# An attention step on one core: scores of block n+2 moved ahead of the values product and the fold

## The chip, the cores and the metric

One core of one Trainium2 chip runs the whole program. The metric is the device time of one execution in microseconds; the median of three executions is 4254.33 us (4252.37 to 4255.28).

## What is computed

Two layers of a hybrid transformer block over 256 context tokens and 1024 latent tokens, width 1024: an input projection, three groups of heads (retention; latent attention, MLA, with 4 heads; grouped-query attention, GQA, with 6 query heads), an output projection, and a gated MLP. The change lies in the two kinds of attention. For each head and each block of 128 queries both compute

```python
s = jnp.einsum('bkgqd,bksd->bkgqs', qi, k).astype(F32) * scale
p = jax.nn.softmax(s, axis=-1).astype(v.dtype)
return jnp.einsum('bkgqs,bkse->bkgqe', p, v)
```

Latent queries see all 1280 keys; context queries see the 256 context keys. In the second (last) layer the context queries are left out.

## The kernel before

`attention` (L489) is called four times: MLA and GQA in each layer. It goes through heads in pairs and through the query blocks of each head, one block of 128 queries at a time, numbered n = 0 to N-1. N is 40 for MLA and 60 for GQA in the first layer (ten blocks per head, the first two of them context blocks with 256 keys), and 32 and 48 in the second (eight blocks per head, all with 1280 keys). That makes 180 blocks, 160 of them with 1280 keys. The operands are split into a high and a low part of type fp32r to keep the precision, so the scores take three matmuls per piece of keys in MLA and two in GQA.

The life of a block n, with the engine and the line:

- **scores** (PE, L554): up to three pieces of 512, 512 and 256 keys into the PSUM buffer S[n % 2]. Each piece waits on `lo_done` of block n-2, whose last reader of the same buffer is `low` (L674).
- **maximum** (DVE, L660): the row maximum, once the scores are complete.
- **exp** (ACT, L620): exponential with the sum of the row, into `probs[n % 2]` in SBUF.
- **transposes** (PE, L564): ten 128x128 transposes (two for a context block), back into the same S[n % 2].
- **high** (ACT, L629): three copies into `pth`, the high part; the first one starts when the first four transposes are done.
- **low** (DVE, L674): a reciprocal of the sum (L666) and three subtractions into `ptl`, each after its piece of `high`. They free S[n % 2] piece by piece for the scores of n+2.
- Two blocks make a group G = n // 2. **values** (PE, L583) multiplies the transposed probabilities of a group with the value matrix: ten matmuls of 256 columns for the high part in the even iteration n = 2G+2, ten for the low part in the odd one. **evacuate** (ACT, L644) copies the result out in iteration 2G+3. **fold_halves** (PE, L591) adds its halves in the even iteration 2G+4, and **normalise** (DVE, L686) scales the result into `o_tok` in the same iteration.
- **flush**: for five (four) iterations of each next pair of heads, two more transposes (PE, L575) and a copy (ACT, L638) bring the finished outputs back to feature order; SyncE stores them.
- **prep** (DVE, L895, L896 for MLA; L1007 for GQA) makes the high parts of the next head's queries and keys, GpSimd (`prep_pool`) the low parts, and in GQA SyncE copies them to the other partitions (`prep_double`). It comes in the iterations n % NS == 2 and n % NS == NH + 2, and `scores` waits for it (`prep_wait`) in the first block of a head.

Each engine has its own program, in an order written by hand, and runs it in that order; semaphores tie them together. In iteration n ACT does high(n), a flush, exp(n+1) and, when n is odd, evacuate. DVE does maximum(n+1), low(n), and, when n is even, normalise and then prep. The order of PE (L597 to L613) is the one that the change touches.

Of the kernel before, what the change touches and what calls it, by code (L numbers as in the profile page):

```python
# [47 lines left out]
def backbone(nc, a):  # L48
# [440 lines left out]
    def attention(s, last, npairs, first_tile, terms, values_of, prep, prep_pool, prep_double, prep_wait):  # L489
# [7 lines left out]
        N = npairs * NS  # L497
# [21 lines left out]
        def head_of(n):  # L519
            return (n % NS) // NH  # L520

        def block_of(n):
            return heads[n % NH]

        def is_ctx(n):
            return block_of(n) < XB

        def pieces(n):

            return [(0, 2)] if is_ctx(n) else [(0, 4), (4, 8), (8, 10)]  # L530
# [3 lines left out]
        def flush_of(n):  # L534

            f = n - NS - FLUSH0
            return (f // NS, f % NS) if f >= 0 and f % NS < NP and f // NS < npairs else None

        @block.tensor
        def _(pe):  # L540
            def scores(n):
                hd, b = head_of(n), block_of(n)
                if n % NH == 0:
                    prep_wait(pe, n // NS, hd)
                for p, (k0, k1) in enumerate(pieces(n)):
                    if n >= 2:
                        if is_ctx(n - 2) and p:

                            pe.wait_ge(lo_done, cut[n - 2] + 1)
                        else:  # L550
                            pe.wait_ge(lo_done, cut[n - 2] + p + 1)
                    c0, w = k0 * P, (k1 - k0) * P
                    for x, (q, k) in enumerate(terms[hd]):
                        mm = nc.tensor.matmul(S[n % 2][:, c0:c0 + w], q[:, b * P:(b + 1) * P], k[:, c0:c0 + w],  # L554
                                              start=(x == 0), stop=(x == len(terms[hd]) - 1))
                mm.then_inc(s_done, 1)

            def transposes(n):
                pe.wait_ge(exp_done, n + 1)
                for k0, k1 in pieces(n):  # L560
                    if k0 == 8 and flush_of(n):
                        flush(n)
                    for b in range(k0, k1):
                        tr = nc.tensor.transpose(S[n % 2][:, b * P:(b + 1) * P], probs[n % 2][:, b * P:(b + 1) * P], ident[:, :])  # L564
                    tr.then_inc(t_done, 1)

            def flush(n):
                g, f = flush_of(n)
                pe.wait_ge(o_done, g * 2 * NP + NP + f + 1)
                if n >= N:  # L570
                    pe.wait_ge(lo_done, cut[N])
                    pe.wait_ge(flushed, max(g * NP + f - 1, 1))
                for j in range(2):
                    b = heads[2 * f + j]
                    tr = nc.tensor.transpose(S[n % 2][:, TOK + j * P:TOK + (j + 1) * P], o_tok[:, b, :], ident[:, :])  # L575
                tr.then_inc(flush_t, 1)

            def values(G, pt, done, n_done, end):
                n = 2 * G
                pe.wait_ge(done, n_done)  # L580
                nk = 2 if is_ctx(n) else BLK
                for k in range(nk):
                    mm = nc.tensor.matmul(O[G % 2][:, :256], values_of(n // NS, head_of(n), k), pt[G % 2][:, k, :],  # L583
                                          start=(not end and k == 0), stop=(end and k == nk - 1))
                if end:
                    mm.then_inc(pv_done, 1)

            def fold_halves(G):
                pe.wait_ge(osb_done, G + 1)
                for j in range(2):  # L590
                    mm = nc.tensor.matmul(O[G % 2][:, 256 + j * HD:256 + (j + 1) * HD], osb[G % 2][:, j * P:(j + 1) * P], fold[:, :],  # L591
                                          start=True, stop=True)
                mm.then_inc(fold_done, 1)
            pe.wait_ge(folder, 1)
            scores(0)
            scores(1)
            for n in range(N + FLUSH0 + NP):  # L597
                if n < N:
                    transposes(n)
                elif flush_of(n):  # L600
                    flush(n)
                G = n // 2 - 1
                if 0 <= G < NG:
                    if n % 2 == 0:
                        if G >= 2:
                            pe.wait_ge(o_done, G - 1)
                        values(G, pth, hi_done, cut[2 * G + 2], False)
                    else:
                        values(G, ptl, lo_done, cut[2 * G + 2], True)
                if n % 2 == 0 and 0 <= G - 1 < NG:  # L610
                    fold_halves(G - 1)
                if n + 2 < N:
                    scores(n + 2)  # L613

        @block.scalar
        def _(act):
# [1223 lines left out]
```

## Time and profile before

| | |
|---|---|
| median of three executions | 4254.33 us |
| the profiled execution, its own time | 4252.16 us |
| span of its profile | 4250.3 us |
| PE matmul busy | 3711.8 us (87%) |
| DVE busy | 2305.8 us (54%) |
| ACT busy | 1327.1 us (31%) |
| GpSimd busy | 873.6 us (21%) |
| mean granted clock of TensorE | 0.937 |
| MLA blocks, first layer | about 674 to 842 us |
| GQA blocks, first layer | about 918 to 1138 us |
| MLA blocks, second layer | about 2884 to 3025 us |
| GQA blocks, second layer | about 3101 to 3290 us |

The four attention stages take together some 17% of the span; all the rest of the program is untouched. PE's rows come in two kinds: LDWEIGHTS (PEld) loads the stationary operand, MATMUL (PE) streams the other. Matmuls overlap, so the duration of a row is longer than the time that it takes of the engine. What an operation costs PE is read from start to start of its LDWEIGHTS rows and those of the next operation; below this is called its slot.

### The profile page before, as it was taken

How to read it: one execution, taken by the hardware profiler on the slowest of the kernel's cores; microseconds unless marked ns; L12 is line 12 of the kernel's file. 1: busy time of each engine (PE TensorE's matmuls, PEld its weight loads, DVE VectorE, ACT ScalarE, POOL GpSimd, SP SyncE). 2: the span in 40 equal slices, each digit the busy share in tenths (PEclk: the TensorE clock that was granted, in tenths of full speed). 3: DMA queues.
4: the chain of work that ended last, by engine and by line, in shares of the span. 5: the costliest groups of instructions: out<-in, count | busy, mean ns of one | idle time of the engine just before them, and what ended most of it. 6: DMA issues, size and time to landing. Idle time of an engine off the chain costs nothing. (4 is left out here: it accounts for less than half of the span.)

```text
span 4250.3 us, 51487 instructions
## 1 busy us (share of the span) xinstructions
PE 3711.8 (87%) x19458; PEld 3097.2 (73%) x19458; DVE 2305.8 (54%) x3122; ACT 1327.1 (31%) x2214; POOL 873.6 (21%) x343
## 2 busy tenths in 40 slices
PE   7999658849797999999999699668689889999997
PEld 6788546838685888888888488538578657777774
DVE  1402457657614555655666611467577256666666
ACT  1322125546613222222221311135557132222222
POOL 0233001000120443343322112002000112233221
PEclk9999869979898999999999899879899889999998
DMA  4233220011220222222210122220110211111111
GB/s 180 81 112 107 71 85 1 13 54 26 77 71 31 65 74 69 59 69 69 69 35 24 41 89 88 74 67 2 47 23 20 83 46 44 44 44 50 51 47 40
DMA packets 113292, 249.16 MB, mean 59 GB/s; under 512 B 11600, under 2 KB 61648, under 8 KB 113040
## 3 DMA queue, kind: packets, MB, share of 16 engines
q1 hardware_dynamic: 104672, 239.22, 17.6%
q10 hardware_dynamic: 8496, 8.26, 0.6%
q8 instruction: 80, 1.31, 0.1%
q14 instruction: 44, 0.36, 0.0%
HBM read 200.39 MB, written 39.98 MB: 57 GB/s over the span
## 5 line engine op out<-in xcount | busy, mean ns | idle before, releaser
L108 POOL TENSOR_TENSOR wlo<-raw,whi 128x1024 fp32r<-128x1024 f32 x267 | 677.8, 2560 | 1101.7 <-ACT whi L97 1101.4
L1648 DVE SCALAR_TENSOR_TENSOR xT<-down_acc,mod,xT 128x512 f32<-128x512 f32 (+1 forms) x880 | 560.3, 696 | 283.2 <-PE down_acc L138 280.7
L136 PE MATMUL up_acc<-h_hi,whi 128*128 128x512 f32 (+1 forms) x1760 | 655.7, 373 | 37.8 <-POOL wlo L108 18.8
L137 PE MATMUL up_acc<-h_lo,whi 128*128 128x512 f32 (+1 forms) x1760 | 649.5, 369 | 0.0
L138 PE MATMUL up_acc<-h_hi,wlo 128*128 128x512 f32 (+1 forms) x1760 | 649.0, 369 | 0.0
L97 ACT ACTIVATE whi<-raw 128x1024 fp32r<-128x1024 f32 x267 | 281.0, 1055 | 587.7 <-PE down_acc L138 412.8
L136 PEld LDWEIGHTS up_acc<-h_hi,whi 128*128 128x128 f32 x1760 | 332.9, 189 | 102.8 <-ACT up L1567 45.6
L138 PEld LDWEIGHTS up_acc<-h_hi,wlo 128*128 128x128 f32 x1760 | 332.5, 189 | 56.2
L137 PEld LDWEIGHTS up_acc<-h_lo,whi 128*128 128x128 f32 x1760 | 332.9, 189 | 53.5 <-issue 0.2
L136 PE MATMUL proj_acc<-h_hi,whi 128*128 128x512 f32 (+1 forms) x936 | 340.7, 364 | 15.7 <-DVE h_lo L335 15.7
L136 PE MATMUL down_acc<-hid_hi,whi 128*128 128x512 f32 (+1 forms) x880 | 333.9, 379 | 20.0 <-POOL hid_lo L1493 20.0
L660 DVE TENSOR_REDUCE negmax<-scores 128x1 f32<-128x1280 f32 (+1 forms) x180 | 247.0, 1372 | 174.2 <-PE scores L554 173.9
L1567 ACT ACTIVATE up<-up_acc 128x512 f32<-128x512 f32 (+1 forms) x220 | 121.5, 553 | 695.2 <-PE up_acc L138 694.8
L1493 POOL TENSOR_TENSOR hid_lo<-y,hid_hi 128x1281 fp32r<-128x1281 f32 (+1 forms) x44 | 117.7, 2676 | 1072.6 <-ACT hid_hi L1578 1072.6
L137 PE MATMUL proj_acc<-h_lo,whi 128*128 128x512 f32 (+1 forms) x936 | 337.9, 361 | 0.0
L138 PE MATMUL proj_acc<-h_hi,wlo 128*128 128x512 f32 (+1 forms) x936 | 337.5, 361 | 0.0
L138 PE MATMUL down_acc<-hid_hi,wlo 128*128 128x512 f32 (+1 forms) x880 | 329.3, 374 | 0.0
L137 PE MATMUL down_acc<-hid_lo,whi 128*128 128x512 f32 (+1 forms) x880 | 329.1, 374 | 0.0
L1627 DVE TENSOR_SCALAR y<-up,convw 128x1281 f32<-128x1281 f32 (+1 forms) x88 | 123.3, 1402 | 353.0 <-ACT up L1567 353.0
L629 ACT ACTIVATE pth<-scores 128x512 fp32r<-128x512 f32 (+1 forms) x500 | 225.9, 521 | 215.6 <-PE scores L564 215.6
L674 DVE TENSOR_TENSOR ptl<-scores,pth 128x512 fp32r<-128x512 f32 (+1 forms) x500 | 264.9, 583 | 16.9 <-ACT pth L629 16.9
L620 ACT ACTIVATE probs<-scores,negmax 128x1280 f32<-128x1280 f32 (+1 forms) x180 | 224.6, 1248 | 85.9 <-DVE negmax L660 85.8
(209 smaller groups left out, 6326.3 us busy)
## 6 DMA issues: line engine op xcount, KB each, us to landing
raw<-in_w_mlp SPq DMA_DIRECT2D x180, 512.0 KB, 3.6
raw<-in_w_proj SPq DMA_DIRECT2D x63, 512.0 KB, 4.2
proj_scratch<-stage SPq DMA_DIRECT2D x33, 640.0 KB, 3.2
raw<-in_w_mix SPq DMA_DIRECT2D x24, 512.0 KB, 4.2
kc<-proj_scratch SPq DMA_DIRECT2D x38, 192.0 KB, 2.6
mix_scratch<-o_feat SPq DMA_DIRECT2D x45, 128.0 KB, 1.7
ada_raw<-in_w_ada SPq DMA_DIRECT2D x10, 512.0 KB, 7.6
xT<-in_xT SPq DMA_DIRECT2D x1, 5120.0 KB, 21.8
```

The lines of the kernel that those rows point to most:

```text
L97: nc.scalar.activation(self.hi[k][:, :], self.raw[k][:, :], ACT.Copy).then_inc(self.hi_ready, 1)
L108: nc.gpsimd.tensor_tensor(self.lo[k][:, :], self.raw[k][:, :], self.hi[k][:, :].bitcast(f32), ALU.subtract).then_inc(self.lo_ready, 1)
L136: nc.tensor.matmul(out, hi, xhi, start=start, stop=False)
L137: nc.tensor.matmul(out, hi, xlo, start=False, stop=False)
L138: return nc.tensor.matmul(out, lo, xhi, start=False, stop=stop)
L620: nc.scalar.activation(probs[n % 2][:, :nk], S[n % 2][:, :nk], ACT.Exp, bias=negmax[:, n:n + 1], accum_out=rsum[:, n:n + 1]).then_inc(exp_ ...
L629: nc.scalar.activation(pth[G % 2][:, k0:k1, j * P:(j + 1) * P], S[n % 2][:, k0 * P:k1 * P].rearrange("p (b q) -> p b q", q=P), ACT.Copy).t ...
L660: nc.vector.tensor_reduce(negmax[:, n:n + 1], S[n % 2][:, :CTX if is_ctx(n) else TOK], AX.X, ALU.max, negate=True).then_inc(max_done, 1)
L674: nc.vector.tensor_tensor(ptl[G % 2][:, k0:k1, j * P:(j + 1) * P], S[n % 2][:, k0 * P:k1 * P].rearrange("p (b q) -> p b q", q=P), pth[G % ...
L1567: nc.scalar.activation(up[half][:, pc:pc + w], ub[c][:, :w], ACT.Copy).then_inc(up_evac, 1)
L1627: nc.vector.tensor_scalar(o, u[:, lo_col:hi_col], cw(1), cw(3), ALU.mult, ALU.add).then_inc(tap, 1)
L1648: nc.vector.scalar_tensor_tensor(xs, db[g % DB][:, :w], mod_of(layer, 5, m, c), xs, ALU.mult, ALU.add).then_inc(added, 1)
```

## The change

In each iteration PE now does the scores of block n+2 directly behind the transposes of block n (or the flush), and the values product and the fold after them. Nothing is added or taken away, and the other engines' programs stay as they are.

```diff
@@ -599,6 +599,8 @@
                     transposes(n)
                 elif flush_of(n):
                     flush(n)
+                if n + 2 < N:
+                    scores(n + 2)
                 G = n // 2 - 1
                 if 0 <= G < NG:
                     if n % 2 == 0:
@@ -609,8 +611,6 @@
                         values(G, ptl, lo_done, cut[2 * G + 2], True)
                 if n % 2 == 0 and 0 <= G - 1 < NG:
                     fold_halves(G - 1)
-                if n + 2 < N:
-                    scores(n + 2)
```

## Rows read from the trace of the kernel before

**Rows 1.** Timeline, one even GQA iteration: start, us, engine, line, operation, what, count, idle before.
```profile
970.61 1.12 PEld L564 LDWEIGHTS scores<-ident,probs 128*128 128x128 f32 x10
970.91 1.49 DVE L660 TENSOR_REDUCE negmax<-scores 128x1 f32<-128x1280 f32 x1 [0.73 <-PE scores L554]
971.41 1.36 ACT L629 ACTIVATE pth<-scores 128x512 fp32r<-128x512 f32 x3 [1.02 <-PE scores L564]
971.70 1.26 PEld L583 LDWEIGHTS values<-pth,gvs 128*128 128x128 f32 x10
...
972.39 1.60 DVE L674 TENSOR_TENSOR ptl<-scores,pth 128x512 fp32r<-128x512 f32 x3
972.65 1.34 ACT L620 ACTIVATE probs<-scores,negmax 128x1280 f32<-128x1280 f32 x1
972.88 0.54 PEld L591 LDWEIGHTS values<-fold,osb 128*128 128x128 f32 x4
...
973.34 0.19 PEld L554 LDWEIGHTS scores<-ks,gqh 128*128 128x128 f32 x1
```

**Rows 2.** Timeline, starts of exp: fourth after that of rows 1, and two in MLA.
```profile
988.06 1.34 ACT L620 ACTIVATE probs<-scores,negmax 128x1280 f32<-128x1280 f32 x1
...
2923.60 1.34 ACT L620 ACTIVATE probs<-scores,negmax 128x1280 f32<-128x1280 f32 x1
...
2958.52 1.34 ACT L620 ACTIVATE probs<-scores,negmax 128x1280 f32<-128x1280 f32 x1
```

**Rows 3.** Page, the costliest groups: busy, mean ns | idle before, releaser.
```profile
L660 DVE TENSOR_REDUCE negmax<-scores 128x1 f32<-128x1280 f32 (+1 forms) x180 | 247.0, 1372 | 174.2 <-PE scores L554 173.9
```

**Rows 4.** Timeline, GQA: a high and the low behind it, when DVE stood idle.
```profile
954.64 1.36 ACT L629 ACTIVATE pth<-scores 128x512 fp32r<-128x512 f32 x3 [0.75 <-PE scores L564]
...
955.27 1.62 DVE L674 TENSOR_TENSOR ptl<-scores,pth 128x512 fp32r<-128x512 f32 x3 [0.87 <-ACT pth L629]
```

**Rows 5.** Timeline, GQA: a low and the scores that wait for it.
```profile
968.59 1.59 DVE L674 TENSOR_TENSOR ptl<-scores,pth 128x512 fp32r<-128x512 f32 x3
...
969.30 0.19 PEld L554 LDWEIGHTS scores<-ks,gqh 128*128 128x128 f32 x1 [1.21 <-DVE ptl L674]
```

**Rows 6.** Timeline, GQA: a fold that normalise (L686) waits for.
```profile
957.86 0.54 PEld L591 LDWEIGHTS values<-fold,osb 128*128 128x128 f32 x4
...
958.57 0.29 DVE L686 TENSOR_TENSOR o_tok<-values,rinv 128x128 f32<-128x128 f32 x1 [0.61 <-PE values L591]
```

**Rows 7.** Timeline, GQA: a normalise, the next maximum, transposes waiting for exp, the values.
```profile
953.73 0.28 DVE L686 TENSOR_TENSOR o_tok<-values,rinv 128x128 f32<-128x128 f32 x1
953.92 0.42 DVE L660 TENSOR_REDUCE negmax<-scores 128x1 f32<-128x256 f32 x1
953.95 1.08 PEld L564 LDWEIGHTS scores<-ident,probs 128*128 128x128 f32 x10 [0.50 <-ACT probs L620]
...
954.99 1.26 PEld L583 LDWEIGHTS values<-ptl,gvs 128*128 128x128 f32 x10
```

**Rows 8.** Timeline, MLA, second layer: scores, prep on DVE, the next maximum and transposes.
```profile
2933.02 0.19 PEld L554 LDWEIGHTS scores<-mkh,mqh 96*128 96x128 f32 x1
...
2933.78 0.68 DVE L895 TENSOR_SCALAR mqh<-mq 96x1024 fp32r<-96x1024 f32 x1
...
2934.77 1.12 PEld L564 LDWEIGHTS scores<-ident,probs 128*128 128x128 f32 x10
...
2935.11 1.48 DVE L660 TENSOR_REDUCE negmax<-scores 128x1 f32<-128x1280 f32 x1
```

**Rows 9.** Timeline, GQA: prep on DVE.
```profile
966.38 0.81 DVE L1007 TENSOR_SCALAR gqh<-gq 64x1280 fp32r<-64x1280 f32 x1
```

**Rows 10.** Windows: the stretch, busy us (and count) per engine, PE clock, DMA, GB/s.
```profile
550.00:600.00 50.00, 31.75 (x152) 26.59 (x151) 33.91 (x74) 9.80 (x17) 0.00 (x0) 0.64 0.29 79
...
997.00:1033.00 36.00, 33.71 (x250) 30.82 (x250) 27.90 (x51) 25.91 (x56) 2.92 (x1) 1.00 0.15 37
```

**Rows 11.** Groups by line: evacuate: count | busy, mean ns | idle before, releasers.
```profile
L644 ACT ACTIVATE osb<-values 128x256 f32<-128x256 f32 x90 | 35.9, 399 | 12.0 <-PE values L583 11.7
```

## The prediction

> **What bounds the attention steps now.** I read the page first (busy shares and the costliest groups), then the groups by line, then the timeline of single iterations in each of the four attention stages, and last the windows for the granted clock. Only `attention` is changed, so only its 180 blocks count. The page shows DVE idle for 174 us ahead of the row maximum, waiting for scores [rows 3]; that is what an earlier issue of the scores could go for. The question is whether DVE's idle time, or something on PE, sets the pitch from block to block. The timeline answers it. In a GQA iteration PE runs the transposes (slot 971.70 - 970.61 = 1.09 us), the values product (972.88 - 971.70 = 1.18), in even iterations the fold (973.34 - 972.88 = 0.46), and the scores [rows 1]. Exp starts are (988.06 - 972.65)/4 = 3.85 us apart in GQA [rows 1, 2] and (2958.52 - 2923.60)/8 = 4.37 us in MLA [rows 2], so a pair of blocks takes 7.70 and 8.74 us. PE's own slots nearly fill that. DVE waits because PE is full; its idle time costs little. The values product lies exactly over the stretch in which ACT and DVE turn the transposes of block n into `pth` and `ptl` and so free S[n % 2] for the scores of n+2.
>
> **The chain that the change uncovers.** From the start of the transposes to the first copy is 971.41 - 970.61 = 0.80 us [rows 1]; from that copy to the first subtraction, when DVE is free, 955.27 - 954.64 = 0.63 [rows 4]; from the subtraction to the first matmul of the scores 969.30 - 968.59 = 0.71 [rows 5]. Together 2.14 us, of which 1.09 are transposes. Now the values product (1.18) and every second time the fold fill the rest, and PE waits only where they are short (1.21 us of idle of PE's weight load in the row at 969.30, where much of the product lay bare [rows 5]). After the change PE has nothing to do there: the scores of n+2 stand at the head of its queue, and the values and the fold wait behind them. Their inputs have been ready for an iteration, but a ready product does not pass a waiting instruction. The trace shows that: at 953.95 the transposes wait 0.50 us for exp, and the ready values product follows only behind them, at 954.99 [rows 7].
> The Trainium skill (TensorE: Matmul & The Clock Gate, "Part 2: What happens when you issue a matmul") says that TensorE's queue pulls weight loads forward past matmuls in flight, and that the matmuls stay in program order. By that rule the product stays behind too; if it could pass, the sum below would be zero.
>
> **The steps, worked out.** Let A be the end of the scores' slot on PE. S is the scores' slot: 970.61 - 969.30 = 1.31 us in GQA, with its waits between pieces [rows 1, 5]; 2934.77 - 2933.02 = 1.75 in MLA [rows 8]. Each iteration goes from one A to the next.
>
> *Even iteration n+2 (its values product and fold come behind its scores, so this interval holds the odd iteration's values product):* values 1.18, transposes to copy 0.80, copy to subtraction 0.63, subtraction to scores 0.71: the scores start at A + 3.32. DVE doesn't delay this: the maximum starts at A + 0.30 (970.91 - 970.61) and lets a subtraction start 972.39 - 970.91 = 1.48 us later [rows 1], at A + 1.78, ahead of the 2.61 that PE's way takes. Interval: GQA 3.32 + 1.31 = 4.63, MLA 5.07.
>
> *Odd iteration (this interval holds the even iteration's values product and its fold):* by PE's way alone 1.18 + 0.46 + 0.80 + 0.63 + 0.71 = 3.78. But DVE's order decides here. Its program has normalise of the even iteration ahead of the next maximum, and normalise needs the fold, which now comes after scores and values. The fold starts at A + 1.18, normalise 958.57 - 957.86 = 0.71 later [rows 6], the maximum 953.92 - 953.73 = 0.19 after that [rows 7] instead of at A + 0.30, the subtraction 1.48 later, the scores 0.71 later: A + 4.27. Queued behind the waiting normalise are prep and the maximum, and for them wait exp and the next subtraction. Interval: GQA 5.58, MLA 6.02.
>
> A pair takes 4.63 + 5.58 = 10.21 us in GQA against 7.70, +2.51; in MLA 5.07 + 6.02 = 11.09 against 8.74, +2.35. Exp stays off the path: the maximum takes 1.49 us and exp 1.34 [rows 1], and the transposes that need them come over 5 us after the scores. Evacuate (ACT, 0.40 us [rows 11]) now ends about A + 1.43 + 0.40 = A + 1.83, if its lag behind the values is that of the fold (0.71 - 0.46 = 0.25); the next copy starts at A + 1.98. It fits, by 0.15 us.
>
> **Counting.** There are 80 pairs of full blocks, 32 in MLA and 48 in GQA. The ten context pairs of the first layer have two transposes, one copy and two values matmuls per part, so both the chain and the product that covered it shrink, and full neighbours gain as much from the short product as the context pair pays for the detour. I count them at nothing, within 1 us each either way (10 us). At each stage's two ends the penalty is missing or partial: no values product in iterations 0 and 1, no normalise before iteration 4, no scores in the last two. That is about five of the steps, 2.5 pairs per stage, chosen from writing out those iterations. So MLA (32 - 5) x 2.35 = 63 us, GQA (48 - 5) x 2.51 = 108 us.
>
> **Prep** comes behind normalise, so on the new path it costs in full: MLA 2935.11 - 2933.78 = 1.33 us [rows 8], GQA 0.81 [rows 9]. There are 16 of them; the first of each stage (iteration 2) has no normalise ahead and is hidden by the scores. 4 x 1.33 + 8 x 0.81 = 12 us. Before, they hid in DVE's idle time. GpSimd's and SyncE's part comes six or more iterations before the head that needs it (the wait for it now stands ahead of a values product too); hidden by over 15 us, at nothing. **Flush:** its two transposes come behind the first eight, so they do not gate the first copy, and its copy on ACT lies beside the first two subtractions: nothing. It lengthens PE's iteration now and may not later, so this can be a few us less.
>
> Sum: 63 + 108 + 12 = 183 us on the profiled execution's 4252 us gives 4435. The median of the runs is 2 us above that execution, within what the runs differ by. I say 4436 us, 4.3% slower. A measurement of this kernel tells 0.2% (8.5 us) from no change, so this is far outside.
>
> **Bounds of the terms.** I lay some 150 intervals; an error of 0.1 us in each is 15 us. If evacuate is late by 0.3 us in each pair, +22 us. The detour over normalise is 4.27 - 3.78 = 0.49 us on some 70 odd intervals, 34 us, with the 12 of prep.
>
> **Rivals.**
> 1. *Normalise doesn't gate* (chance 0.09). If PE's way ends last in odd iterations too, the penalty is 34 + 12 us less: about 4389. Against it: DVE's program has a single order, and normalise at 958.57 did wait for the fold [rows 6].
> 2. *One more wait* (0.14). Evacuate or the later pieces of the subtraction end behind what I lay out, 0.2 to 0.4 us per interval: 4460 to 4490. The margin of 0.15 us speaks for it.
> 3. *The clock falls* (0.03). TensorE now idles about 1 us per even interval and 1.5 per odd one. In the retention stretch 550 to 600 us, with PE busy 31.75 of 50 us, the granted clock was 0.64, between its two levels of 1.2 and 2.4 GHz; in a GQA stretch with idle gaps in most iterations, PE busy 33.71 of 36, it stayed at 1.00 [rows 10]. I expect a busy share of about three quarters, so between these. At the low level PE's slots double: the values and scores alone add 1.2 + 1.2 us per interval, about 400 us more, 4800 and above; partly fallen, some tens. The Trainium skill (the same page, "A second HAM failure mode: psum-queue depth-cycling") says that idles between groups of matmuls, if frequent enough, make the clock swing between its levels. It would give this case; the trace of before, with shorter idles, does not.
> 4. *Faster* (0.02). Maxima come earlier relative to the transposes and the waits of the scores for `ptl` vanish. That needs the low part of block n to be ready when its transposes end. It decides only if the chain of 2.14 us were shorter than the 1.09 of the transposes. If it held, PE would run back to back; a pair's slots in GQA are 2 x (1.09 + 1.18 + 1.2) + 0.46 = 7.4 against 7.70, 14 us in 48 pairs: 4238.
> 5. *No change* (0.02): PE gets to the values while the scores wait, or the pitch is set elsewhere: 4252.
>
> My forecast has 0.70 (4400 to 4460 within it). The range of 4385 to 4480 takes in rival 1 and most of rival 2. Faster 0.02, same 0.02, slower 0.96.
>
> **What would show it.** In the changed trace: PE idle about 1 us ahead of each scores in even and 1.5 in odd iterations, released by DVE `ptl` (some 200 us under L554); normalise idle ahead, released by PE's fold, and the maximum starting about 2.1 us after the scores in odd iterations and 0.3 in even ones; exp starts alternating near 4.6 and 5.6 us in GQA, 5.1 and 6.0 in MLA; the clock at 1.00 inside the stages; all else unchanged. A stage pitch under 4.0 us in GQA, or maxima directly behind scores in all iterations, would prove me wrong.

## The result and the profile after

The changed kernel takes 4462.01 us (median of four executions, 4455.03 to 4470.24) against 4253.35 us for the kernel before in the same runs: ratio 1.0493, interval 1.0471 to 1.0515. It is 209 us slower. The forecast was 4436, within 4385 to 4480. All ratios rest on fast executions; the only slow one is one of the twelve of the split fold (below), with 8387.73 us.

The profiled execution took 4465.69 us with a span of 4463.9, 213.6 more than before. The first and last exp of each attention stage show where: first layer MLA 203.2 us against 158.4 and GQA 277.9 against 212.7, second layer MLA 173.9 against 134.4 and GQA 244.6 against 181.6. The four sum to 212.4 us. The stretches before, between and behind them are each within 5 us of what they were, and 1.2 us longer in all.

The page of the changed kernel: busy us, share of the span, instructions.

```profile
PE 3761.1 (84%) x19458; PEld 3112.9 (70%) x19458; DVE 2314.6 (52%) x3122; ACT 1337.7 (30%) x2214; POOL 873.2 (20%) x343
```

The groups by line of the changed kernel, for the maximum, normalise, and the first matmul of the scores in GQA and MLA: busy, mean ns | idle before, releasers.

```profile
L660 DVE TENSOR_REDUCE negmax<-scores 128x1 f32<-128x1280 f32 (+1 forms) x180 | 246.3, 1368 | 129.0 <-PE scores L554 128.8
L686 DVE TENSOR_TENSOR o_tok<-values,rinv 128x128 f32<-128x128 f32 x90 | 26.2, 291 | 196.9 <-PE values L591 196.9
L554 PE MATMUL scores<-ks,gqh 128*128 128x512 f32 (+1 forms) x300 | 130.4, 435 | 188.6 <-DVE ptl L674 119.1 <-DMA gql<-gql 69.2
L554 PE MATMUL scores<-mkh,mqh 96*128 96x512 f32 (+1 forms) x200 | 81.1, 406 | 95.0 <-DVE ptl L674 78.2 <-POOL mkl L903 16.5
```

The same two kinds of group in the kernel before:

```profile
L686 DVE TENSOR_TENSOR o_tok<-values,rinv 128x128 f32<-128x128 f32 x90 | 25.5, 284 | 18.0 <-PE values L591 18.0
L554 PE MATMUL scores<-ks,gqh 128*128 128x512 f32 (+1 forms) x300 | 122.1, 407 | 86.6 <-DMA gql<-gql 69.3 <-DVE ptl L674 17.2
L554 PE MATMUL scores<-mkh,mqh 96*128 96x512 f32 (+1 forms) x200 | 78.9, 395 | 28.9 <-POOL mkl L903 16.5 <-DVE ptl L674 12.3
```

The idle time ahead of the maximum, which an earlier issue of the scores should cut, did fall, from 174 us [rows 3] to 129. By itself it gave nothing: the pitch got longer all the same. The waits that do hold it grew: PE for `ptl` ahead of the scores from 17.2 + 12.3 to 119.1 + 78.2 us, normalise for the fold from 18.0 to 196.9.

One pair of GQA blocks in the changed kernel (timeline, the counterpart of [rows 1, 5, 6]; start, us, engine, line, what, idle before):

```profile
3331.00 1.34 ACT L620 ACTIVATE probs<-scores,negmax 128x1280 f32<-128x1280 f32 x1
...
3332.49 1.26 PEld L583 LDWEIGHTS values<-pth,gvs 128*128 128x128 f32 x10
3333.68 0.53 PEld L591 LDWEIGHTS values<-fold,osb 128*128 128x128 f32 x4
3334.07 1.13 PEld L564 LDWEIGHTS scores<-ident,probs 128*128 128x128 f32 x10
3334.39 0.29 DVE L686 TENSOR_TENSOR o_tok<-values,rinv 128x128 f32<-128x128 f32 x1 [2.30 <-PE values L591]
3334.59 1.48 DVE L660 TENSOR_REDUCE negmax<-scores 128x1 f32<-128x1280 f32 x1
3334.83 1.36 ACT L629 ACTIVATE pth<-scores 128x512 fp32r<-128x512 f32 x3 [2.40 <-PE scores L564]
...
3336.06 1.60 DVE L674 TENSOR_TENSOR ptl<-scores,pth 128x512 fp32r<-128x512 f32 x3
3336.11 1.33 ACT L620 ACTIVATE probs<-scores,negmax 128x1280 f32<-128x1280 f32 x1
3336.78 0.19 PEld L554 LDWEIGHTS scores<-ks,gqh 128*128 128x128 f32 x1 [1.58 <-DVE ptl L674]
...
3338.07 1.27 PEld L583 LDWEIGHTS values<-ptl,gvs 128*128 128x128 f32 x10
3338.39 1.49 DVE L660 TENSOR_REDUCE negmax<-scores 128x1 f32<-128x1280 f32 x1 [0.73 <-PE scores L554]
3339.29 1.11 PEld L564 LDWEIGHTS scores<-ident,probs 128*128 128x128 f32 x10
3339.59 0.39 ACT L644 ACTIVATE osb<-values 128x256 f32<-128x256 f32 x1 [2.06 <-PE values L583]
...
3340.09 1.36 ACT L629 ACTIVATE pth<-scores 128x512 fp32r<-128x512 f32 x3
3340.79 1.62 DVE L674 TENSOR_TENSOR ptl<-scores,pth 128x512 fp32r<-128x512 f32 x3 [0.83 <-ACT pth L629]
3341.32 1.34 ACT L620 ACTIVATE probs<-scores,negmax 128x1280 f32<-128x1280 f32 x1
3341.53 0.19 PEld L554 LDWEIGHTS scores<-ks,gqh 128*128 128x128 f32 x1 [1.12 <-DVE ptl L674]
```

The scores' slot ends at 3332.49. In this odd interval the fold starts 1.19 us later, normalise at + 1.90, the maximum at + 2.10, the first subtraction at + 3.57, the next scores at + 4.29. In the even interval that follows, from 3338.07, the maximum starts at + 0.32 and is done by + 1.81, 0.21 us before the first copy starts; the scores start at + 3.46. The pair takes 3341.32 - 3331.00 = 10.32 us. PE's weight load stands idle 1.58 and 1.12 us in it; between matmuls the same two waits are 1.34 and 0.89 us (the MATMUL rows at 3336.79 and 3341.53).

### The profile page after: what moved, and what is told of

It is laid out like the page before. It is cut to its first block and busy times, and to the rows that moved or that the text cites. A ratio compares the mean times of both kernels' runs of the same rounds, so it can differ in the third digit from the quotient of the medians.

```text
span 4463.9 us, 51487 instructions
## 1 busy us (share of the span) xinstructions
PE 3761.1 (84%) x19458; PEld 3112.9 (70%) x19458; DVE 2314.6 (52%) x3122; ACT 1337.7 (30%) x2214; POOL 873.2 (20%) x343
## 5 line engine op out<-in xcount | busy, mean ns | idle before, releaser
L554 PE MATMUL scores<-ks,gqh 128*128 128x512 f32 (+1 forms) x300 | 130.4, 435 | 188.6 <-DVE ptl L674 119.1
```

## The experiments

All ratios are against the kernel before, run on the same chip. Differences to the changed kernel take its 4462.01 us from the section above. The pitch of a pair is read off two exp starts that lie three GQA pairs apart, the same blocks of the second layer in each kernel. The kernel before gives 23.07/3 = 7.69 there:

```profile
3249.55 1.36 ACT L620 ACTIVATE probs<-scores,negmax 128x1280 f32<-128x1280 f32 x1
...
3272.62 1.34 ACT L620 ACTIVATE probs<-scores,negmax 128x1280 f32<-128x1280 f32 x1
```

The changed kernel gives 30.83/3 = 10.28. This is a little less than the 10.32 of the pair above, because the stretch holds one shorter step:

```profile
3455.80 1.35 ACT L620 ACTIVATE probs<-scores,negmax 128x1280 f32<-128x1280 f32 x1
...
3486.63 1.33 ACT L620 ACTIVATE probs<-scores,negmax 128x1280 f32<-128x1280 f32 x1
```

**One: only the fold behind the scores.** `scores(n + 2)` between the values product and the fold:

```diff
@@ against the kernel before, PE
+                if n + 2 < N:
+                    scores(n + 2)
                 if n % 2 == 0 and 0 <= G - 1 < NG:
                     fold_halves(G - 1)
-                if n + 2 < N:
-                    scores(n + 2)
```

> The order of the kernel before with only the fold moved behind the scores; the values product still lies between transposes and scores. Theory (two costs, the uncovered chain and the detour over normalise): no part of the chain of 2.14 us is uncovered, but the maximum of the next block waits for fold and normalise, so it starts about 0.9 us after the scores instead of 0.3 in odd intervals. The scores start at A + 3.09 instead of A + 2.73, 0.36 us on some 70 intervals, and prep costs its 12 us: 37 us, near 4290. Rival (only the place of the values product counts): 4253.

Measured: 4297.33 us, ratio 1.0102 (1.0085 to 1.0119), 46 us slower than before, where 37 were expected. The rival's 4253 is out.

**Two: only the values product behind the scores.**

```diff
@@ against the kernel before, PE
                 G = n // 2 - 1
+                if n % 2 == 0 and 0 <= G - 1 < NG:
+                    fold_halves(G - 1)
+                if n + 2 < N:
+                    scores(n + 2)
                 if 0 <= G < NG:
...
-                if n % 2 == 0 and 0 <= G - 1 < NG:
-                    fold_halves(G - 1)
-                if n + 2 < N:
-                    scores(n + 2)
```

> The fold stays ahead of the scores, only the values product is moved behind them. Theory: the chain from transposes to scores is uncovered in every interval (3.32 us to the start of the scores in both), normalise does not hold the maximum. A pair takes 9.3 us in GQA and 10.1 in MLA, 105 us in all, near 4358, and the idle stretches are too short for the clock to fall. Rival (the uncovered chain is small, the fold and normalise make the loss): below 4300.

Measured: 4365.56 us, ratio 1.0262 (1.0245 to 1.0279), 114 us slower, where 105 were expected. In its trace the clock never falls inside the attention stages.

**Three: the changed kernel, normalise after the maximum.**

```diff
@@ against the changed kernel, DVE
-                if n % 2 == 0 and 0 <= n // 2 - 2 < NG:
+                if n % 2 == 1 and 0 <= n // 2 - 2 < NG:
                     normalise(n // 2 - 2)
```

> The changed kernel, with normalise one iteration later in the program of DVE (odd instead of even iterations), so that it comes behind the maximum it held up. Theory: odd intervals shrink by 0.49 us and prep by its 12 us, and the idle stretches of over 2 us are gone and the clock falls with them: 4462 - 34 - 12 - up to 25, so 4390 to 4415. Rival (the order on PE alone sets the pitch): 4462, unchanged.

Measured: 4392.19 us, ratio 1.0327 (1.031 to 1.0344), 70 us less than the changed kernel.

The exp starts of these three, two rows each. First the fold alone, 24.39/3 = 8.13 us for a pair:

```profile
3297.25 1.36 ACT L620 ACTIVATE probs<-scores,negmax 128x1280 f32<-128x1280 f32 x1
...
3321.64 1.33 ACT L620 ACTIVATE probs<-scores,negmax 128x1280 f32<-128x1280 f32 x1
```

The values product alone, 27.86/3 = 9.29:

```profile
3362.68 1.35 ACT L620 ACTIVATE probs<-scores,negmax 128x1280 f32<-128x1280 f32 x1
...
3390.54 1.35 ACT L620 ACTIVATE probs<-scores,negmax 128x1280 f32<-128x1280 f32 x1
```

Both moved, normalise later, 29.01/3 = 9.67:

```profile
3384.04 1.36 ACT L620 ACTIVATE probs<-scores,negmax 128x1280 f32<-128x1280 f32 x1
...
3413.05 1.35 ACT L620 ACTIVATE probs<-scores,negmax 128x1280 f32<-128x1280 f32 x1
```

And normalise by its group in the same three kernels. With the fold alone behind the scores it waits 114 us:

```profile
L686 DVE TENSOR_TENSOR o_tok<-values,rinv 128x128 f32<-128x128 f32 x90 | 26.2, 291 | 114.2 <-PE values L591 113.6
```

With the values product alone behind them, 16:

```profile
L686 DVE TENSOR_TENSOR o_tok<-values,rinv 128x128 f32<-128x128 f32 x90 | 25.3, 281 | 16.0 <-PE values L591 16.0
```

With both moved and normalise later, 16 as well:

```profile
L686 DVE TENSOR_TENSOR o_tok<-values,rinv 128x128 f32<-128x128 f32 x90 | 25.2, 280 | 16.1 <-PE values L591 16.1
```

So there are two costs, and they are not additive. The product alone behind the scores costs 114 us. When the fold goes behind them too, with normalise out of the maximum's way, the chain loses that cover as well: 141 us, 27 more, by the pitch 9.67 - 9.29 = 0.38 us per pair. And normalise ahead of the maximum adds 70 us, more than the 46 of experiment one. By the pitch it is 10.28 - 9.67 = 0.61 us per pair against 8.13 - 7.69 = 0.44 with the fold alone, so about 14 of the 24 us more, on 80 pairs. These 70 hold the cost of prep and of the clock too: behind idle stretches the clock falls twelve times in the changed kernel (below), three times with the fold alone, and never with normalise later. 114 + 27 + 70 = 211; each term is the difference of one kernel to the next, so the sum must come out at the whole loss, and the 2 us to 209 are only those of the kernel before in other runs.

**Four: half of the product ahead of the scores.** `values` takes a part (0: the first half of its matmuls, 1: the rest):

```diff
@@ against the changed kernel, PE
+                G = n // 2 - 1
+                if 0 <= G < NG:
+                    if n % 2 == 0:
+                        if G >= 2:
+                            pe.wait_ge(o_done, G - 1)
+                        values(G, pth, hi_done, cut[2 * G + 2], False, 0)
+                    else:
+                        values(G, ptl, lo_done, cut[2 * G + 2], True, 0)
                 if n + 2 < N:
                     scores(n + 2)
...
-                        values(G, pth, hi_done, cut[2 * G + 2], False)
+                        values(G, pth, hi_done, cut[2 * G + 2], False, 1)
...
-                        values(G, ptl, lo_done, cut[2 * G + 2], True)
+                        values(G, ptl, lo_done, cut[2 * G + 2], True, 1)
```

> The changed kernel with the first five of the ten matmuls of each values product put back ahead of the scores. Theory (each matmul ahead of the scores covers the chain for its own slot): both intervals of a pair are 0.59 us shorter, 1.18 us on some 70 pairs, 83 us, and the clock falls less often because every idle stretch is shorter, up to 20 us: 4360 to 4380. Rival (the cover counts only when the whole product is ahead, for instance because scores still come after the product's end in PE's queue): above 4420.

Measured: 4364.09 us, ratio 1.0258 (1.0243 to 1.0273), 98 us less than the changed kernel. The pair, 27.24/3 = 9.08 us, is 1.20 us shorter than 10.28, two times five slots of 0.12 us:

```profile
3359.76 1.35 ACT L628 ACTIVATE probs<-scores,negmax 128x1280 f32<-128x1280 f32 x1
...
3387.00 1.33 ACT L628 ACTIVATE probs<-scores,negmax 128x1280 f32<-128x1280 f32 x1
```

For these five matmuls cover counted for its own slot, and half of the product brought back nearly half of the loss. A part of the 98 us is the clock, which falls only five times here. The other five count for less: the changed kernel with the whole product ahead is the kernel of experiment one, 9.08 - 8.13 = 0.95 us per pair below this one, where their slots are again 1.2. So cover is worth its slot only as long as the path that it covers ends last.

**Five: useless work where PE is idle.**

```diff
@@ against the changed kernel, PE
+            def filler(n):
+                G = n // 2 - 1
+                pe.wait_ge(o_done, G - 1 + n % 2)
+                for j in range(12 if n % 2 else 8):
+                    nc.tensor.transpose(O[(G + n) % 2][:, 384:512], ident[:, :], ident[:, :])
...
+                if 6 <= n and n + 2 < N:
+                    filler(n)
                 if n + 2 < N:
                     scores(n + 2)
```

> The changed kernel, with useless transposes of the identity between transposes and scores (8 in even iterations, 12 in odd ones, about 0.9 and 1.3 us), where PE stands idle. They write a part of the values bank that nobody reads. Theory (a part of the loss above the forecast is the clock, which falls at the longest idle stretches): the added work is hidden, the granted clock in the attention stages goes to 1.00, and the time falls by 10 to 25 us, to about 4440 to 4450. Rival (the clock is no part of it): unchanged or slower, 4462 or above.

Measured: 4451.04 us, ratio 1.0464 (1.0447 to 1.0482), 11 us less than the changed kernel, with 1480 more transposes on PE. The intervals of the two ratios overlap a little (1.0471 against 1.0482), so the median of whole runs alone would not carry this. The profiles do. The pair is the same, 3471.65 - 3440.85 = 30.80, /3 = 10.27 us against 10.28. The difference lies in single steps behind a prep or a context block. In the changed kernel one GQA step behind a prep took 3364.69 - 3357.61 = 7.08 us from exp to exp, with the filler 3351.01 - 3345.41 = 5.60. The windows show why. First the MLA prep at 3061.6 in the changed kernel; columns: the window, busy us and count on PE, PEld, DVE, ACT and GpSimd, then TensorE's granted clock, DMA and GB/s.

```profile
3061.00:3063.00 2.00, 1.49 (x15) 1.25 (x13) 1.56 (x4) 1.12 (x3) 0.53 (x1) 1.00 0.00 0
3063.00:3065.00 2.00, 0.00 (x0) 0.00 (x0) 2.00 (x4) 0.75 (x2) 2.00 (x1) 1.00 0.00 0
3065.00:3067.00 2.00, 1.83 (x8) 1.53 (x9) 1.04 (x3) 0.91 (x2) 2.00 (x2) 0.88 0.00 0
3067.00:3069.00 2.00, 2.00 (x11) 2.00 (x11) 1.35 (x1) 0.00 (x0) 1.16 (x1) 0.50 0.03 8
3069.00:3071.00 2.00, 1.99 (x14) 1.74 (x13) 0.21 (x2) 0.96 (x3) 0.00 (x0) 0.77 0.00 0
```

The scores behind that prep, in the timeline of the changed kernel:

```profile
3065.17 0.50 PE L554 MATMUL scores<-mkh,mqh 96*128 96x512 f32 x1 [2.67 <-DVE ptl L674]
...
3067.20 2.25 PEld L583 LDWEIGHTS values<-ptl,mvs 128*128 128x128 f32 x10
```

PE has no matmul for 2.67 us; its clock then falls from 2.4 to 1.2 GHz (1.00 to 0.50) while it works again, and the ten values matmuls take 2.19 us (to the transposes at 3069.39) instead of 1.18. A whole stretch with a GQA prep, in the changed kernel:

```profile
3351.00:3380.00 29.00, 22.79 (x150) 19.75 (x150) 16.94 (x28) 15.92 (x34) 2.34 (x1) 0.94 0.15 37
```

The same stretch with the filler:

```profile
3340.00:3370.00 30.00, 28.87 (x218) 25.67 (x216) 18.48 (x32) 16.22 (x33) 2.35 (x1) 1.00 0.14 37
```

The filler did not keep the clock up everywhere: at two MLA preps, where 1.37 and 1.50 us without a matmul were left, it fell all the same. Step by step, from exp to exp, the two traces can be compared over all four stages. Ten steps are shorter with the filler, each by 1.47 to 1.55 us; they are the ones behind a fall that the filler prevented. Eight steps, at context blocks, are longer by 0.28 or 0.29 us, by all appearance the filler's own cost. In the changed kernel the clock falls twelve times behind an idle stretch (not counting one fall early in the first stage, which the kernel before has too, and one at the start of the last, where no filler runs). At 1.5 us each that is some 18 us (an estimate), of which the filler gave back 15 and took 2; the two falls that stayed are counted like the ten.

**Six to nine: half of the fold in each iteration, and a later reciprocal.** In the kernel before PE waits some 0.2 us for the first subtraction in odd iterations, and has the fold to spare in even ones. So half of the fold goes to each: `fold_half(G, j)` does the matmul of half j, and normalise comes when both are done:

```diff
@@ against the kernel before, PE and DVE
-                if n % 2 == 0 and 0 <= G - 1 < NG:
-                    fold_halves(G - 1)
+                if 0 <= G - 1 < NG:
+                    fold_half(G - 1, n % 2)
...
-                if n % 2 == 0 and 0 <= n // 2 - 2 < NG:
+                if n % 2 == 1 and 0 <= n // 2 - 2 < NG:
                     normalise(n // 2 - 2)
```

> A version meant to beat the kernel before: its order, with one half of the fold in the even iteration and the other in the odd one, and normalise in the odd iteration. Theory (the rest that PE still waits for in odd iterations, 0.2 us before the scores, is filled by half a fold, 0.23 us): a pair falls by 0.1 us in GQA and 0.23 in MLA, 11 us in all, 4241. Rival (the chain over maximum and low on DVE sets both intervals anyway): 4252.

Measured: 4248.52 us against 4253.58, ratio 0.9988 (0.998 to 0.9997). The pair, 22.78/3 = 7.59 us, is 0.10 shorter, as laid out:

```profile
3247.41 1.36 ACT L621 ACTIVATE probs<-scores,negmax 128x1280 f32<-128x1280 f32 x1
...
3270.19 1.35 ACT L621 ACTIVATE probs<-scores,negmax 128x1280 f32<-128x1280 f32 x1
```

The gain, 5 us, is half of what was expected. The control, with the second hunk alone:

> The kernel before with normalise one iteration later, alone: the control for the two runs that move normalise. Theory: in the kernel before the fold comes ahead of the scores, so normalise holds nothing up and its place counts for nothing: 4252, within 5 us. Rival (normalise also costs time in the kernel before): faster by 10 us or more.

Measured: 4258.31 us, ratio 1.0011 (1.0002 to 1.002). So a later normalise seems to cost 5 us in the order of before; by the profiles the four stages are 3.0 us longer, nearly all in the first layer, where the context blocks are (GQA from first to last exp 215.4 us against 212.7; the second layer's two stages do not grow). Why it costs there was not followed up. The split of the fold itself would then be worth about 10 us by the medians, 4258 to 4248, or 6.6 by the four stages of the profiles.

The last two put the reciprocal behind the subtractions of `low`, where nothing waits for it:

```diff
@@ DVE, low(n)
-                nc.vector.reciprocal(rinv[:, n:n + 1], rsum[:, n:n + 1]).then_inc(own, 1)
...
                                             pth[G % 2][:, k0:k1, j * P:(j + 1) * P].bitcast(f32), ALU.subtract).then_inc(lo_done, 1)
+                nc.vector.reciprocal(rinv[:, n:n + 1], rsum[:, n:n + 1]).then_inc(own, 1)
```

> The version with the split fold, and the reciprocal of low behind its three subtractions instead of ahead of them. Theory (in GQA the scores of both iterations now start when the first subtraction behind the maximum lets them, so the 0.07 us between the starts of reciprocal and first subtraction lie on the chain): 0.14 us per GQA pair, 7 us, and nothing in MLA, where PE is full: 4242. Rival (PE's slots set both): 4248, unchanged.

> The kernel before with the reciprocal behind the subtractions, alone. Theory: only the odd intervals, where PE waits 0.2 us for the first subtraction, gain 0.07 us each, 80 of them at most: 4248. Rival (PE-bound throughout): 4253.

Measured: 4247.69 us (0.9987, 0.9978 to 0.9996) with the split fold, 4248.85 (0.9988, 0.9979 to 0.9997) alone, against 4253.38. By the pitch, the kernel with both has (3270.63 - 3248.11)/3 = 7.51 us per GQA pair, 0.08 below the split fold, of the 0.14 expected. The 7 us that it should gain on the split fold do not show in the medians (4247.69 against 4248.52). The reciprocal alone came out at its 4248.

Whole runs cannot tell the three versions from each other. Each is some 5 us, 0.12%, below the kernel before, at the edge of what can be measured: the intervals reach up to 0.9997.

## Why the prediction was right

The path, the direction and the range held. The size did not quite: 4462 is 26 us above the forecast and 2 us above the 4400 to 4460 that it gave itself 0.70 for. The number lies where rival 2 (one more wait) put it, but that mechanism is not what the trace shows: evacuate ends at 3339.59 + 0.39 = 3339.98, 0.11 us before the next copy, and the scores' slot with its waits between pieces is 1.29 us, no longer than before. What is missing is small errors of the steps and rival 3, the clock, at its small price ("partly fallen, some tens"). Point by point:

- **What bounds.** Right where the forecast needed it: the maximum's idle time fell by 45 us and the kernel lost 209, and experiments two and four show the values product as the cover of the chain over ACT and DVE. That PE's slots set the pitch before holds for the even iterations. In the odd GQA ones it was already the round trip over DVE:

```profile
3216.02 1.11 PEld L564 LDWEIGHTS scores<-ident,probs 128*128 128x128 f32 x10
...
3216.32 1.49 DVE L660 TENSOR_REDUCE negmax<-scores 128x1 f32<-128x1280 f32 x1 [0.61 <-PE scores L554]
...
3217.80 1.60 DVE L674 TENSOR_TENSOR ptl<-scores,pth 128x512 fp32r<-128x512 f32 x3
...
3218.52 0.19 PEld L554 LDWEIGHTS scores<-ks,gqh 128*128 128x128 f32 x1 [0.16 <-DVE ptl L674]
```

  From the end of the scores' slot (3216.02) the maximum, the first subtraction behind it and the next scores follow at + 0.30, + 1.78 and + 2.50; PE's transposes and values product are done at + 2.26 (the product's slot is 1.18 from 3217.10). This is the 0.2 us that experiments six to nine went for.
- **The even interval.** The scores were laid out at A + 3.32; they start at + 3.46 in the timeline above. Transposes to copy is 3340.09 - 3339.29 = 0.80 as laid out; three terms are some hundredths longer than in the rows that I took: the values' slot 1.22 instead of 1.18, copy to subtraction 0.70 instead of 0.63, subtraction to scores 0.74 instead of 0.71.
- **The odd interval.** A + 4.27 against + 4.29: the detour over normalise, step for step. Experiment three shows its price, by the pitch 10.28 - 9.67 = 0.61 us per pair, where 0.49 stood. The detour came out as laid, but the way without it is shorter: with normalise later the scores start at 3393.71 - 3390.01 = A + 3.70, not 3.78.
- **The pair.** 10.21 forecast and 10.32 measured in GQA, 11.09 and 11.23 in MLA (exp starts at 3147.53 and 3169.99, two pairs apart). On the 43 and 27 pairs that I counted, this is 5 and 4 us more. One sign that I named did not show: the exp starts do not alternate near 4.6 and 5.6 us but are 5.11 and 5.21 us apart (5.57 and 5.65 in MLA). The scores do alternate (ends 3332.49 and 3338.07, 5.58 us; starts 3336.78 and 3341.53, 4.75). Exp follows the late maximum in one interval (maximum at 3334.59 + 1.48, exp at 3336.11) and ACT's three copies in the other (first copy 3340.09, exp 3341.32), which evens it out.
- **The ends of the stages.** I took five intervals per stage as free of the penalty. In the second layer's MLA stage the intervals are long from the fourth on (3.40, 3.87, 4.26, 5.45, 5.10 us and so on), so it is rather three to four; about 7 us over the four stages.
- **Context pairs.** Counted at nothing, and near it: with the filler, where the clock falls only twice, the first layer's stages lose 41.3 and 60.5 us against the kernel before, the second's 38.6 and 59.2. Of the 4 us more, 2 are probably the filler's own.
- **Prep.** Two of the MLA preps lengthen their step by 1.3 us (6.90 against 5.57 and 5.62), the 1.33 forecast. In GQA a step grows by 0.60 where 0.81 stood; on the eight counted this is 2 us less.
- **The clock.** This step failed. I let it stand at 1.00 and gave its fall 0.03. It fell, though not over whole stages: only behind stretches of 1.95 us and more without a matmul, at preps and context blocks, where the uncovered chain meets the detour or a prep. It cost some 18 us, of which experiment five gave 15 back. The Trainium skill's section that I cited for this rival ("A second HAM failure mode: psum-queue depth-cycling" in TensorE: Matmul & The Clock Gate) says that frequent short idles make the clock swing. In steady pairs, with 1.34 and 0.89 us between matmuls in each, it stayed at 1.00; so the trace agrees only for the longer ones.

183 + 9 + 7 - 2 + 18 = 215 us, against 212.4 in the four stages of the profiles and 209 by the medians. That it closes to within a few us is no proof of each share: those of the latencies, of the ends and of prep were read from the traces, not tested one by one, and the 18 is an estimate.

## What to carry to other kernels

When an engine's order is changed to feed a consumer sooner, look first at what the moved work lay behind: a product that looks as if it delays the next step may be the cover of a round trip over two other engines. It is then worth its own slot, up to the point where another path ends last: here five of ten matmuls gave their full slots, the other five 0.95 of 1.2 us. Then follow each instruction that was pushed back to whoever waits for it in an in-order program: the fold is 0.46 us of work, but with it normalise moved, and with normalise the maximum that had nothing to do with it. If the consumer's wait is not what sets the pitch, shortening it gives nothing. And when two traces are compared by their pitch, take both over the same blocks.

## What was not expected of the hardware

TensorE's clock fell from 1.00 to 0.50 after 2.67 us without a matmul, at a prep, some 1.3 us into the work that followed, and after 1.95 us at a context block. Adding 1480 useless transposes to the program made it some 11 us faster. The stretches of 0.9 and 1.3 us in every steady pair did not move the clock. The length of the stretch alone does not tell: of the twenty stretches of over 1.9 us without a matmul in the changed kernel's attention stages twelve were followed by a fall and eight (1.93 to 2.23 us) were not, and with the filler the clock fell behind 1.37 and 1.50 us. What decides was not found here.
